# Attention in pairs of heads with turned values, and four scalings of the probabilities per pair and branch on GpSimd

## What is computed

```python
# nsa_mixer: 8 query heads, 2 key/value groups, three branches, gates g (8 x 3)
out = g[0] * softmax(q k_c' / 8) v_c      # 15 compressed blocks of keys
    + g[1] * softmax(q k_slc' / 8) v_slc  # causal, all 256 tokens
    + g[2] * softmax(q k_win' / 8) v_win  # causal, window 512 (all tokens)
# moba_mixer: 8 heads, causal, own keys and values
y_b = softmax(q_b k_b' / 8) v_b
```

## Time and profile before

| | us |
|---|---|
| runs before, median (lowest to highest) | 2434.91 (2433.66 to 2440.22) |
| the profiled execution, its own time | 2438.09 |
| its span, first to last instruction | 2436.2 |
| mean granted clock of TensorE, share of full | 0.916 |
| attention stage, layer 0 (1542.44 to 1620.38) | 77.94 |
| attention stage, layer 1 (2060.66 to 2136.47) | 75.81 |

### The profile page before, as it was taken

The page is one execution under the profiler, slowest core; times in us unless marked ns, Lnnn a source line. Parts: engine busy times, 40 slices in busy tenths (PEclk is TensorE's granted clock), DMA queues, the critical chain, the costliest instruction groups (busy, mean ns, idle before and its releaser), DMA issues.

```text
span 2436.2 us, 28154 instructions
## 1 busy us (share of the span) xinstructions
PE 2034.8 (84%) x12190; PEld 1308.8 (54%) x12190; DVE 411.6 (17%) x1137; ACT 325.4 (13%) x737; POOL 0.2 (0%) x4
## 2 busy tenths in 40 slices
PE   6999997766656666666666699989999999899999
PEld 4468786421111111221111347878888658788887
DVE  4213343200000000000000114431000114411000
ACT  2232020200000000000000112431000122501000
POOL 0000000000000000000000000000000000000000
PEclk9999998888787788888788899899999999999999
DMA  9247577599999999999999954216334545045341
GB/s 327 77 165 271 197 267 285 210 422 427 430 428 429 428 428 429 428 429 427 430 428 429 411 195 157 86 70 242 138 127 168 192 138 208 1 173 207 136 175 35
DMA packets 147872, 648.48 MB, mean 266 GB/s; under 512 B 10645, under 2 KB 17410, under 8 KB 123016
## 3 DMA queue, kind: packets, MB, share of 16 engines
q1 hardware_dynamic: 140754, 643.00, 66.6%
q10 hardware_dynamic: 7030, 4.18, 0.7%
HBM read 646.10 MB, written 1.05 MB: 266 GB/s over the span
## 4 chain that ended last, share of the span: by engine, by line
PE 62%; DMA 31%; DVE 3%; ACT 2%; issue 1%; ACTq 1%; SPq 0%; DVEq 0%
DMA ring<-in_w_exp 31%; PE bank L806 27%; PE bank L820 6%; PE bank L2268 6%; PE bank L1601 4%; PE bank L1365 4%; PE bank L1616 2%; PE bank L577 1%; PE bank L839 1%; PE bank L684 1%; DMA ring<-in_w_branch_ml 1%; ACTq L346 1%; PE bank L1289 1%; PE bank L2074 1%; PE bank L2067 1%
## 5 line engine op out<-in xcount | busy, mean ns | idle before, releaser
L806 PE MATMUL bank<-hx,ring 128*128 128x256 f32 (+1 forms) x2944 | 655.1, 385 | 0.7 <-ACT hx L702 0.7
L806 PEld LDWEIGHTS bank<-hx,ring 128*128 128x128 f32 x2944 | 559.4, 190 | 93.3 <-issue 19.0
L1601 PE MATMUL bank<-ring,arena 128*32 128x512 f32 x1968 | 307.3, 759 | 201.8 <-DMA ring<-in_w_exp 191.4
L1601 PEld LDWEIGHTS bank<-ring,arena 128*32 128x32 f32 x1968 | 60.8, 124 | 430.9 <-DMA ring<-in_w_exp 310.0
L1616 PE MATMUL bank<-ring,arena 128*32 128x512 f32 x1008 | 159.9, 774 | 83.5 <-DMA ring<-in_w_exp 72.7
L820 PE MATMUL bank<-ring,hx 128*128 128x512 f32 (+1 forms) x384 | 152.9, 560 | 1.1 <-ACT hx L762 0.7
L2268 PE MATMUL bank<-arena,ring 128*128 128x256 f32 x704 | 152.4, 379 | 1.5 <-DVE arena L2301 1.5
L2268 PEld LDWEIGHTS bank<-arena,ring 128*128 128x128 f32 x704 | 133.6, 190 | 20.0 <-issue 1.9
L1616 PEld LDWEIGHTS bank<-ring,arena 128*32 128x32 f32 x1008 | 32.3, 130 | 193.6 <-DMA ring<-in_w_exp 114.5
L820 PEld LDWEIGHTS bank<-ring,hx 128*128 128x128 f32 x384 | 72.8, 190 | 80.1 <-issue 76.4
L1659 DVE COPY arena<-bank 128x256 f32<-128x256 f32 x16 | 6.8, 424 | 523.1 <-PE bank L1606 523.1
(11 more groups left out here) (370 smaller groups left out, 1542.3 us busy)
## 6 DMA issues: line engine op xcount, KB each, us to landing
ring<-in_w_exp SPq DMA_DIRECT2D x186, 2048.0 KB, 16.2
ring<-in_w_ada SPq DMA_DIRECT2D x36, 2048.0 KB, 12.4
ring<-in_w_in SPq DMA_DIRECT2D x29, 2048.0 KB, 9.1
ring<-in_w_ffn_in SPq DMA_DIRECT2D x20, 2048.0 KB, 7.9
ring<-in_w_ffn_out SPq DMA_DIRECT2D x10, 2048.0 KB, 7.8
ring<-in_w_out SPq DMA_DIRECT2D x6, 2048.0 KB, 12.0
arena<-in_w_exp SPq DMA_DIRECT2D x4, 2048.0 KB, 16.1
ring<-in_w_up_nsa SPq DMA_DIRECT2D x2, 2048.0 KB, 9.4
```

The costliest lines, as they stand in the source:

```text
L806: ins = pe.matmul(b[:, o:o + n], w[:, k, j * P:(j + 1) * P], h[:, k, :], start=k == 0, stop=k == KD - 1)
L1601: ins = pe.matmul(banks[s][32 * j:32 * j + 32, :], e_xe[:, 2 * t + kk, :], w[:, kk, 512 * j:512 * j + 512], start=t + kk == 0, stop=t + kk ...
```

## The change

Heads go in pairs. The 24 heads become 12 pairs `m`, in the order MoBA pairs 4 to 7, then for each pair 0 to 3 the selected and the window branch. `kT` holds the keys of two heads, one on partitions 0 to 63 and one on 64 to 127, and `scores(m)` runs one matmul per head on its half of TensorE's rows, into two banks. `values(m)` is turned: the values are the stationary operand and the probabilities stream, each head has its half of the columns, and the output has the head's columns on partitions, as `mixer_out` wants it in `yT2`. So `y2`, its transposes and their copies go. For that the probabilities have to be divided by their sums and multiplied with the gate ahead of the values: `normed(m)` on VectorE makes the weights, and `pool_attend` on GpSimd applies them in place, in four `tensor_scalar` a pair (two heads, two chunks of query tokens). `turned(m)` waits for GpSimd. The selected and the window branch and the compressed one add up in the same bank. The copies of the turned probabilities go to ScalarE, but for the second head of every third pair, which VectorE copies (`on_dve`). The scale of 1/8 goes into the query gains, and the maxima are taken negated, so that VectorE's `tensor_scalar` L2190 goes. The compressed branch is done for four pairs at once, with scores of 32 columns of TensorE each.

The diff, without context and without the removed lines of `heads`, `attend` and the layout that stand in the functions above:

```diff
-    PE, AC, DV, SP = (Steps(n, K) for n in ("pe", "act", "dve", "sp"))
+    PE, AC, DV, SP, PO = (Steps(n, K) for n in ("pe", "act", "dve", "sp", "pool"))
...
-    kp = view(arena, 9136, P, 16, N)
...
+    kT = view(arena, 9136, P, 8, N)
+    sC = view(arena, 11184, P, 2, 2, 4, 32)
+    scT = view(arena, 11696, P, 2, N)
+    ptc = view(arena, 12208, P, 2, N)
+    vc4 = view(arena, 12720, P, 2, HD)
+    kct = view(arena, 12848, P, 2, 32)
...
-    ptc = view(arena, 17328, 16, 16, P)
...
-    kct = view(arena, 21552, P, 4, 16)
...
-    sums = view(arena, 22308, P, NC, 24)
-    wts = view(arena, 22356, P, NC, 8)
-    sC = view(arena, 22372, P, 16, 16)
...
+    sums = view(arena, 22308, P, 12, 2, 2)
+    wts = view(arena, 22372, P, 12, 2, 2)
...
-    sm = view(scr, 0, P, 3, 384)
-    pt = view(scr, 1152, P, 3, 384)
...
+    sm = view(scr, 0, P, 3, 2, 384)
+    pt = view(scr, 2304, P, 2, 2, 384)
...
-        v.memset(kct, 0.0).then_inc(*DV.step())
+        v.tensor_scalar(gain_l[:, :, 0::2, :], gain_l[:, :, 0::2, :], HD ** -0.5, None, ALU.mult).then_inc(*DV.step())
...
-        for s in range(2):
-            for g in range(2):
-                o = (2 * s + g) * HD
-                ins = pe.matmul(b[0:15, o:o + HD], hidc[:, s, 16 * g:16 * g + 15], cw2[:, l, s, :], start=True, stop=True)
+        for g in range(2):
+            pe.matmul(b[0:15, g * HD:(g + 1) * HD], hidc[:, 0, 16 * g:16 * g + 15], cw2[:, l, 0, :], start=True, stop=True)
+        ins = pe_cvalues(pe, l, bank(pe, f"cval{l}"))
...
+    def pe_cvalues(pe, l, b):
+        for g in range(2):
+            for i in range(4):
+                ins = pe.matmul(b[32 * i:32 * i + 16, g * HD:(g + 1) * HD], hidc[:, 1, 16 * g:16 * g + 16], cw2[:, l, 1, :],
+                                start=True, stop=True)
+        return ins
...
-        v.tensor_copy(kcv[0:15], b[0:15, 0:256].rearrange("p (a b) -> p a b", a=4)).then_inc(*DV.step(f"free cout{l}"))
-        v.wait_ge(*DV.last())
+        v.tensor_copy(kcv[0:15, 0:2, :], b[0:15, 0:128].rearrange("p (a b) -> p a b", a=2)).then_inc(*DV.step(f"free cout{l}"))
+        v.wait_ge(*DV.last())
+        for i in range(4):
+            v.tensor_copy(vc4[32 * i:32 * i + 16], bank_of(f"cval{l}")[32 * i:32 * i + 16, 0:128].rearrange(
+                "p (a b) -> p a b", a=2)).then_inc(*DV.step(f"free cval{l}", f"cval ready{l}"))
...
-        for par in range(2):
-            lo, hi = 64 * par, 64 * par + 64
-            v.tensor_copy(kct[lo:hi, par::2, 0:15], bb[lo:hi]).then_inc(*DV.step(f"free kct{l}", f"kct ready{l}"))
+        v.tensor_copy(kct[:, :, 0:15], bb).then_inc(*DV.step(f"free kct{l}", f"kct ready{l}"))
...
+                s0 = 4 if q == 2 else 0
+                v.tensor_copy(kT[:, s0:s0 + 4, c * P:(c + 1) * P], b[:, :].rearrange("p (i t) -> p i t", i=4)).then_inc(
+                    *DV.step("free " + key, f"kT{l}"))
+    UNITS = [(2, p) for p in range(4, 8)] + [(b, p) for p in range(4) for b in range(2)]
+    LAST = len(UNITS) - 1
+    def obank(key, pair):
+        book.bank[key] = 6 + pair % 2
+        return book.bank[key]
...
+        pe.wait_ge(*at(f"kT{l}"))
+        def scores(m):
+            br, pair = UNITS[m]
+            slot_ = pair if br == 2 else 2 * br + pair // 2
+            b = [bank(pe, f"s{l}_{m}{par}") for par in range(2)]
+            for c in range(NC):
+                for par in range(2):
+                    r = slice(64 * par, 64 * par + 64)
+                    o = slice(0, P) if c == 0 else slice(P, 3 * P)
+                    ins = pe.matmul(b[par][:, o], qT[r, pair, c * P:(c + 1) * P], kT[r, slot_, 0:(c + 1) * P],
+                                    start=True, stop=True)
+                    if c:
+                        ins.then_inc(*PE.step(f"full s{l}_{m}{par}"))
+        def turned(m):
+            for par in range(2):
+                b = bank(pe, f"pt{l}_{m}{par}")
+                pe.wait_ge(*at(f"N{l}_{m}{par}"))
+                for i in range(3):
+                    ins = pe.transpose(b[:, i * P:(i + 1) * P], sm[:, m % 3, par, i * P:(i + 1) * P], ident[:, :])
+                ins.then_inc(*PE.step(f"full pt{l}_{m}{par}"))
+        def values(m):
+            br, pair = UNITS[m]
+            key = f"o{l}_{pair}"
+            n = obank(key, pair)
+            b = claim(pe, n, key) if br != 1 else banks[n]
+            vcol = [(896, 1152, 2328)[br] + ((2 * (pair - 4) + par) if br == 2 else pair // 2) * HD for par in range(2)]
+            for par in range(2):
+                pe.wait_ge(*at(f"PT{l}_{m}{par}"))
+            for c in range(NC):
+                for par in range(2):
+                    o = b[64 * par:64 * par + 64, c * P:N]
+                    p_ = pt[:, m % 2, par, 0:N] if c == 0 else pt[:, m % 2, par, N:N + P]
+                    ins = pe.matmul(o, qkv[:, c, vcol[par]:vcol[par] + HD], p_, start=c == 0 and br != 1, stop=True,
+                                    skip_group_check=True)
+            ins.then_inc(*PE.step(f"V{l}_{m}"))
+            if br == 1:
+                for par in range(2):
+                    ins = pe.matmul(b[64 * par:64 * par + 64, 0:N], vc4[32 * pair:32 * pair + 16, pair // 2, :],
+                                    ptc[32 * pair:32 * pair + 16, par, :], start=False, stop=True, skip_group_check=True)
+                ins.then_inc(*PE.step("full " + key))
+            elif br == 2:
+                book.where["full " + key] = PE.now
+        scores(0)
...
+        bc = [bank(pe, f"cs{l}{par}") for par in range(2)]
+        for p in range(4):
+            for par in range(2):
+                r = slice(64 * par, 64 * par + 64)
+                ins = pe.matmul(bc[par][32 * p:32 * p + 32, 0:N], kct[r, p // 2, :], qT[r, p, :], start=True, stop=True)
+        ins.then_inc(*PE.step(f"full cs{l}"))
+        scores(1)
+        pe.wait_ge(*at(f"scT{l}"))
+        b = bank(pe, f"ct{l}")
+        for par in range(2):
...
+                o = (2 * par + c) * P
+                ins = pe.transpose(b[:, o:o + P], scT[:, par, c * P:(c + 1) * P], ident[:, :])
+        ins.then_inc(*PE.step(f"full ct{l}"))
...
+        scores(2)
+        turned(1)
+        values(0)
+        scores(3)
+        pe.wait_ge(*at(f"NC{l}"))
+        b = bank(pe, f"cp{l}")
+        for par in range(2):
+            for c in range(NC):
+                o = (2 * par + c) * P
+                ins = pe.transpose(b[:, o:o + P], sC[:, par, c].rearrange("p a n -> p (a n)"), ident[:, :])
+        ins.then_inc(*PE.step(f"full cp{l}"))
+        for m in range(2, LAST):
+            turned(m)
+            values(m - 1)
+            if m == 4:
+                pe.wait_ge(*at(f"ptc{l}"))
+                pe.wait_ge(*at(f"cval ready{l}"))
+            if m + 2 <= LAST:
+                scores(m + 2)
+        turned(LAST)
+        values(LAST - 1)
+        values(LAST)
...
+        def probs(m):
+            for par in range(2):
+                act.wait_ge(*at(f"sm{l}_{m}{par}"))
+                for c, (lo, hi) in enumerate(((0, P), (P, 3 * P))):
+                    x = sm[:, m % 3, par, lo:hi]
+                    act.activation(x, x, ACT.Exp, bias=mx[:, m % 3, par, c:c + 1], scale=-1.0,
+                                   accum_out=sums[:, m, par, c:c + 1]).then_inc(*AC.step(f"P{l}_{m}{par}"))
+        def copies(m):
+            for par in range(2):
+                if on_dve(m, par):
+                    continue
+                key = f"pt{l}_{m}{par}"
+                act.wait_ge(*at("full " + key))
+                if m >= 2:
+                    act.wait_ge(*at(f"V{l}_{m - 2}"))
+                act.copy(pt[:, m % 2, par, :], bank_of(key)[:, 0:384]).then_inc(*AC.step("free " + key, f"PT{l}_{m}{par}"))
+        probs(0)
+        act.wait_ge(*at(f"full cs{l}"))
+        for par in range(2):
+            act.copy(scT[:, par, :], bank_of(f"cs{l}{par}")[:, 0:N]).then_inc(*AC.step(f"free cs{l}{par}", f"scT{l}"))
+        probs(1)
...
+        act.activation(sC[:, :, :, :, 0:16], sC[:, :, :, :, 0:16], ACT.Exp).then_inc(*AC.step(f"PC{l}"))
+        for m in range(2, LAST + 1):
+            copies(m - 2)
+            probs(m)
+            if m == 2:
+                act.wait_ge(*at(f"full cp{l}"))
+                act.copy(ptc.rearrange("p a t -> p (a t)"), bank_of(f"cp{l}")[:, :]).then_inc(*AC.step(f"free cp{l}", f"ptc{l}"))
+        copies(LAST - 1)
+        copies(LAST)
...
+    def on_dve(m, par):
+        return par == 1 and m % 3 == 2
+    def pool_attend(g, l):
+        PO.stage("attend")
+        for m in range(LAST + 1):
+            g.wait_ge(*at(f"weights{l}_{m}"))
+            for par in range(2):
+                for c, (lo, hi) in enumerate(((0, P), (P, 3 * P))):
+                    x = sm[:, m % 3, par, lo:hi]
+                    g.tensor_scalar(x, x, wts[:, m, par, c:c + 1], None, ALU.mult).then_inc(*PO.step(f"N{l}_{m}{par}"))
...
+        def softmax_in(m):
+            if m >= 3:
+                v.wait_ge(*at(f"full pt{l}_{m - 3}1"))
+            for par in range(2):
```

(160 more changed lines are left out.)

108 lines of the change are left out of this document (2 added, 106 removed).

## The result

The changed kernel takes 2504.47 us (median of 4 runs, 2502.91 to 2507.33) against 2437.53 us of the kernel before beside it. The ratio is 1.0273, interval 1.0254 to 1.0291: slower by 67 us. Forecast were 2458 us and a range up to 2495. The direction was right, the size was not: a third of the loss was foreseen. The forecast was added to 2434.9 us, the median of the runs that were there then; to 2437.5 it would have made 2461.

A forecast was written before the change was run, and what follows sets the result against it. Attention stages bound by a ring of waits, 3.91 us per two heads, becoming 5.67 us a pair in series; 0.35 us at the upper clock plus 22.8 for the lower gave +23.2, 2458 us, range 2430 to 2495.

The forecast's parts named there:

- The ring: Attention stage: turned, values, scores, softmax_in, normed, four scalings in series, skipping no pair; 5.67 us a pair against 3.91.
- GpSimd's four over 2.2 us: Sign of being wrong: the four scalings of a pair on GpSimd take under 1.2 or over 2.2 us.
- its 5.7 to 7.1: Sign of being right: start-to-start of turned(m) in the attention stage of 5.7 to 7.1 us.
- Four scalings ... I take 1.6 us, near ScalarE: GpSimd's scalings in each pair's pitch: 1.6 us, with 1.12 and 3.56 kept for the range.
- The upper bound of 3.56 us: Dearest case for GpSimd's four scalings a pair: twice ScalarE's 1.78 us on these shapes.
- its rival: GpSimd is the long term: its scalings take 2.6 us a pair, 2482 us, or 3.56, 2505 us; chance 0.18.
- the one of no overlap: Rival: TensorE's halves don't run beside each other, 1.42 us more a pitch; 2465 to 2508 us, between them 2487; chance 0.10.
- I take two thirds of the work at the lower level: TensorE's clock in the attention stage: pauses in every pitch put two thirds of the work at 1.2 GHz, 22.8 us together.
- the last third of 34.2 us: Lower-clock cost in both attention stages, 17.1 us a layer, of which the forecast counted only two thirds.
- 7.12: Pitch of a pair in us with TensorE at the lower clock: 5.67 + 2 x 0.58 + 0.29.
- The clock rival: TensorE's clock stays up in the attention stage despite the pauses: +0.35 us, 2435 us; chance 0.13.
- the faster one: Rival: GpSimd scales at VectorE's pace, 1.12 us a pair, and the clock stays up: 2424 us; chance 0.19.

The follow-up runs named there:

- both edits: Changed kernel with normed(m) ahead of softmax_in(m+1) on VectorE and the four scalings on VectorE instead of GpSimd: 2410.2 us, ratio 0.9887 to the kernel before.

## Why the prediction was right and wrong

**Right: the mechanism.** The ring was read from the two orders of the code before a run, link by link, and the chain after shows these links. Moving one call took its cost away. That TensorE's own saving lies inside a longer ring held too: even without the scalings the changed kernel comes out at 0.9982 of the one before. Two of the prediction's own signs of being wrong came true: GpSimd's four over 2.2 us, and a plain pitch (8.78 us) above its 5.7 to 7.1.

**Wrong: the step "Four scalings ... I take 1.6 us, near ScalarE".** It measured 2.99. The row of a fill tells of no rate, and then ScalarE was chosen as the nearest; GpSimd takes 1.7 times ScalarE's 1.78 us on these shapes. Twenty-four passes make 24 x 1.39 = 33.4 us. The upper bound of 3.56 us held, and its rival was there, with a chance of 0.18. That this rival's dearest case (2505) and the one of no overlap (2508) lie next to the measured 2504.5 is luck: neither of their conditions came true. The fills were misread too: each takes 0.10 us and they overlap, so a quarter of 0.2 is not the time of one; nothing hung on it.

**Wrong: the step "I take two thirds of the work at the lower level".** The stage was at 0.57, that is 2 x 0.57 - 1 = 14% of the time at the upper level, part of it at its two ends, and in the pitch shown above the granted clock is 0.50 throughout. If all of the ring ran at the lower level, the last third of 34.2 us is missing, 11.4 us; if 14% of it ran at the upper, 6.6 us. The two errors are not independent: a longer GpSimd is a longer pause of TensorE. The rivals were priced one by one at a fixed clock, and the range was drawn over them singly, and their sum, 23.2 + 33.4 and 6.6 to 11.4, that is 63.2 to 68.0 us or 2498 to 2503, lay outside it. The stages measured 69.2.

**The small terms.** The pitch by the prediction's own sum at the lower level, with 2.99 us for GpSimd, is 7.12 + 1.39 = 8.51 us against 8.78; over some 21 pitches that is 5.7 us. Added to 63.2 to 68.0 it makes 68.9 to 73.7 against 69.2: the account closes at its lower end, and with the whole 11.4 us it would be too much. Three transposes behind a wait cost 0.87, not 0.64. Values and scores with their two changes of grouping were put at 2 x 1.29 + 0.30 = 2.88 and took 3.11. That halves run beside each other held for row groups as for column groups: at the upper level 0.86 us for two heads' scores, where one head's cost 0.71. So the rival of no overlap is out. The clock rival and the faster one were far off.

**The Trainium skill's figure.** By the 1.8 cycles of the Trainium skill's "GPSIMD Engine Reference", section "Performance versus the Vector engine", the four would have taken an estimated 1.15 us. The trace has 2.99, 2.6 times that, and decides. The same page of the Trainium skill names VectorE for elementwise work on a tile (section "Engine selection"); the scalings on VectorE, which take a third of the time, agree.

## What to carry to other kernels

Write down each engine's order and count, for the operation that an engine waits for, how many turns of the loop lie on the ring that comes back to it; a call placed one line too late in one queue took a skipped turn away and cost as much here as the whole change. After each cure look for the ring again: with both edits the limit was a new one, without TensorE. Before work goes to an engine whose rate no row shows, price its dearest bound together with the lower clock, not each alone, because here a longer wait of TensorE also made its next work slower. When a change looks bad, try its links singly: the same edit with another order and another engine was 1.1% faster than before, and 3.8% under the version as written.

## What the runs showed that was not expected

- GpSimd's float32 `tensor_scalar` costs 0.60 us for 128 columns and 0.92 us for 256; a line through the two is 2.5 ns a column and 0.28 us fixed. VectorE does the four in 1.01 us.
- Matmuls whose results nobody reads made the kernel faster: 8 us with both edits, 31 us in the changed kernel. They hold TensorE's clock, 0.58 to 1.00 in the stage.
- A stage whose pauses came in every pitch had a clock of 0.57, while in the kernel before a single pause (2116 to 2119, busy for 0.63 of 3 us) had left it at 1.00.
